# Expert products of U in three rounded products, with GpSimd making the low parts

## The reference, cut to what matters

```python
def peer(x, w_query, sub_keys, expert_u, expert_v):
    ...
        best_s, best_j = lax.top_k(cand_s, PK_TOPK)
        experts = jnp.take_along_axis(cand_i, best_j, axis=-1)
        gates = jax.nn.softmax(best_s, axis=-1).astype(xb.dtype)
        act = jax.nn.gelu(jnp.einsum('thkd,td->thk', expert_u[experts], xb), approximate=False)
        return jnp.einsum('thk,thkd->td', gates * act, expert_v[experts])
```

## Time and profile before

| | us |
|---|---|
| median of 3 runs | 5192.61 |
| lowest and highest | 5158.98, 5197.61 |
| span of the profiled execution | 5087.9 |
| U part, first gather to last row (in the span) | 2826 to 4254 |
| V part, first product to last | 4266 to 5058 |

### The profile page before, as it was taken

The page is one execution under the profiler, slowest core; times in us unless marked ns, Lnnn a source line. Parts: engine busy times, 40 slices in busy tenths (PEclk is TensorE's granted clock), DMA queues, the critical chain, the costliest instruction groups (busy, mean ns, idle before and its releaser), DMA issues. The chain is left out here.

```text
span 5087.9 us, 68117 instructions
## 1 busy us (share of the span) xinstructions
PE 4732.6 (93%) x27237; PEld 3798.3 (75%) x27237; DVE 3153.2 (62%) x4952; ACT 1249.9 (25%) x1562; POOL 1567.5 (31%) x1385
## 2 busy tenths in 40 slices
PE   8999999999978888899999899999999938899997
PEld 7999999999976555898789555555555526677776
DVE  2323443333436666433457588889778876888987
ACT  2212323233322222322354000000000003334433
POOL 0110000000014444000000222256655564788850
PEclk9999999999988899999999999999999969999998
DMA  5533333233339998524556899999999999999995
GB/s 192 200 141 115 99 107 108 94 111 102 102 110 344 352 355 301 185 106 173 174 206 224 324 421 418 405 410 394 386 395 397 395 387 355 411 408 407 409 407 199
DMA packets 346087, 1377.05 MB, mean 271 GB/s; under 512 B 85396, under 2 KB 128692, under 8 KB 220200
## 3 DMA queue, kind: packets, MB, share of 16 engines
q0 software_dynamic: 138464, 727.19, 35.7%
q1 hardware_dynamic: 176536, 613.34, 32.8%
q10 hardware_dynamic: 30768, 32.11, 1.9%
HBM read 1277.05 MB, written 111.66 MB: 273 GB/s over the span
## 5 line engine op out<-in xcount | busy, mean ns | idle before, releaser
L2262 PE MATMUL i_ps<-f_xT,i_ut 128*128 128x384 f32 x4096 | 1326.6, 487 | 83.6 <-DMA i_ut<-in_u_tiles 83.6
L2262 PEld LDWEIGHTS i_ps<-f_xT,i_ut 128*128 128x128 f32 x4096 | 779.9, 191 | 628.4 <-issue 89.1
L300 PE MATMUL a_acc<-a_xh,a_wh 128*128 128x288 f32 x3104 | 673.2, 299 | 19.1 <-DVE a_xl L526 13.7
L300 PE MATMUL a_acc<-a_xh,a_wl 128*128 128x288 f32 x3104 | 666.4, 296 | 0.0
L300 PE MATMUL a_acc<-a_xl,a_wh 128*128 128x288 f32 x3104 | 665.6, 296 | 0.0
L2674 POOL DMA_INDIRECT i_row<-in_expert_v,f_ei x320 | 481.6, 1505 | 245.2 <-DVE i_sum L2511 97.2
L2511 DVE SCALAR_TENSOR_TENSOR i_ps<-i_row,i_cf,i_ps 128x2048 f32<-128x2048 f32 x190 | 447.5, 2355 | 136.1 <-DMA i_row<-in_expert_v,f_ei 127.0
L300 PEld LDWEIGHTS a_acc<-a_xh,a_wh 128*128 128x128 f32 x3104 | 500.4, 189 | 30.6 <-issue 28.4
L300 PEld LDWEIGHTS a_acc<-a_xl,a_wh 128*128 128x128 f32 x3104 | 501.6, 189 | 0.0
L300 PEld LDWEIGHTS a_acc<-a_xh,a_wl 128*128 128x128 f32 x3104 | 501.4, 189 | 0.0
L2502 DVE CUSTOM_DVE_ANT_0 i_row<-i_row,i_ps 128x2048 f32<-128x2048 f32 x192 | 430.4, 2284 | 98.2 <-DMA i_row<-in_expert_u,f_ei 95.8
(11 more groups left out here) (372 smaller groups left out, 7342.7 us busy)
## 6 DMA issues: line engine op xcount, KB each, us to landing
i_ut<-in_u_tiles SPq DMA_DIRECT2D x128, 1024.0 KB, 9.6
i_ut<-in_expert_v SPq DMA_DIRECT2D x128, 1024.0 KB, 13.1
a_w<-in_w_in SPq DMA_DIRECT2D x97, 1024.0 KB, 5.0
f_w<-in_w_out SPq DMA_DIRECT2D x32, 1024.0 KB, 4.9
f_w<-in_w_query SPq DMA_DIRECT2D x32, 1024.0 KB, 5.2
tmp_Ha<-i_ho ACTq DMA_DIRECT2D x128, 192.0 KB, 9.1
tmp_uT<-a_out POOLq DMA_DIRECT2D x65, 288.0 KB, 2.3
tmp_Wd<-in_zeros SPq DMA_DIRECT2D x16, 1024.0 KB, 7.3
```

The source lines that it names most:

```text
L300: last = nc.tensor.matmul(acc[:, 2 * slot + h, 0:HALF], weights[:, wslot, k * P:(k + 1) * P], x[:, k, h * HALF:(h + 1) * HALF], start=(k = ...
L2262: last = nc.tensor.matmul(p_h[:, e % 2, 0:ND], ut[:, e % RU, k * P:(k + 1) * P], xT[:, k, :], start=(k == 0), stop=(k == KT - 1))
```

## The change

U's dense product is made like V's, as three rounded products. x is split once into `i_xh` (ACT) and `i_xl` (DVE). Of each U tile ACT makes the high part `i_uh` in two halves of 1024 columns (`split_u`, two buffers), and POOL subtracts it from the tile, in place: `i_ul` is the same memory as `i_ut` (`split_low`). PE waits for POOL's halves. POOL's subtractions for tile e stand in its queue behind gather 3(e - 1) + 1. To make room, row buffers go from eight to five and U slots from six to four, and the V part's buffers lie over those of the U part.

```diff
-    R = 8
+    R = 5
-    RU = 6
+    RU = 4
...
+        uh = sb("i_uh", [P, 2, KT * P], F32R)
+        ut, = over(("i_ut", [P, RU, KT * P], F32))
+        ul = sb("i_ul", [P, RU, KT * P], F32R)
...
                     if e < RV:
-                        sp.wait_ge(e_done, NE + (-6, -5, -2, -1)[e] + 1 + 4)
+                        sp.wait_ge(e_done, NE - RU + e + 1 + 4)
...
-                        if e == NE - 6:
+                        if e == NE - RU:
                             sp.wait_ge(routed, 4)
                             sp.wait_ge(placed, 16 * 2 * PICKS)
...
-                        pe.wait_ge(ut_in[e % RU], 16 * (e // RU + 1))
                         for k in range(KT):
-                            last = nc.tensor.matmul(p_h[:, e % 2, 0:ND], ut[:, e % RU, k * P:(k + 1) * P], xT[:, k, :],
-                                                    start=(k == 0), stop=(k == KT - 1))
+                            if k % 8 == 0:
+                                pe.wait_ge(ul_out, 2 * e + k // 8 + 1)
+                            if e == 0 and k % 4 == 0:
+                                pe.wait_ge(xl_out, k // 4 + 1)
+                            hi, lo = uh[:, e % 2, k * P:(k + 1) * P], ul[:, e % RU, k * P:(k + 1) * P]
+                            for t, (u, x) in enumerate(((hi, xh), (hi, xl), (lo, xh))):
+                                last = nc.tensor.matmul(p_h[:, e % 2, 0:ND], u, x[:, k, :], start=(k == 0 and t == 0),
+                                                        stop=(k == KT - 1 and t == 2))
...
                     nc.scalar.copy(ho[:, m, :], p_h[:, e % 2, 0:ND]).then_inc(h_out, 1)
+                    if e + 2 < NE:
+                        split_u(e + 2)
...
+                def split_u(e):
+                    act.wait_ge(ut_in[e % RU], 16 * (e // RU + 1))
+                    if e >= 2:
+                        act.wait_ge(e_done, e - 1 + 4)
+                    for h in range(2):
+                        part = slice(h * D // 2, (h + 1) * D // 2)
+                        nc.scalar.copy(uh[:, e % 2, part], ut[:, e % RU, part]).then_inc(uh_out, 1)
...
+                def split_low(e):
+                    for h in range(2):
+                        part = slice(h * D // 2, (h + 1) * D // 2)
+                        pool.wait_ge(uh_out, 2 * e + h + 1)
+                        nc.gpsimd.tensor_tensor(ul[:, e % RU, part], ut[:, e % RU, part], uh[:, e % 2, part], ALU.subtract
+                                                ).then_inc(ul_out, 1)
...
+                def splits(m):
+                    if m % 3 == 1:
+                        split_low(m // 3 + 1)
...
                 for k in range(PICKS):
                     gather(k, io["expert_u"], ei[:, 0, k:k + 1])
+                    if k == 0:
+                        split_low(0)
+                    splits(k)
...
                 for k in range(PICKS):
                     gather(first_v[0] + k, io["expert_v"], ei[:, 0, k:k + 1])
+                    splits(first_v[0] + k)
                     scatters(first_v[0] + k)
```

More of the change, by code:

```diff
@@ L2091, in peer @@
         tcol = sb("i_tcol", [P, 3])
[L2092 to L2096, removed]
+        vh, vl, gb = over(("i_vh", [P, 2, D], F32R), ("i_vl", [P, 2, D], F32R), ("i_gb", [P, 2, D], F32))
+        xl = sb("i_xl", [P, KT, ND], F32R)
+        ho = sb("i_ho", [P, 4, ND])
+        xh = sb("i_xh", [P, KT, ND], F32R)
+        uh = sb("i_uh", [P, 2, KT * P], F32R)
+        ut, = over(("i_ut", [P, RU, KT * P], F32))
+        ul = sb("i_ul", [P, RU, KT * P], F32R)
         row = sb("i_row", [P, R, D])
+        sb("i_x1_gap", [P, 512])
         sb("i_x1_room", [P, 2, D])
@@ L2115, in peer @@
         ut_in = [tl.sem(f"i_ut_in{k}") for k in range(RU)]
+        xh_out = tl.sem("i_xh_out")
+        xl_out = tl.sem("i_xl_out")
+        uh_out = tl.sem("i_uh_out")
+        ul_out = tl.sem("i_ul_out")
         e_done = tl.sem("i_e_done")
@@ L2178, in load_v @@
                     if e < RV:
-                        sp.wait_ge(e_done, NE + (-6, -5, -2, -1)[e] + 1 + 4)
+                        sp.wait_ge(e_done, NE - RU + e + 1 + 4)
                     else:
                         sp.wait_ge(vl_out, e - RV + 1)
-                    sp.dma_start(ut[:, (e + 2) % RV, :], v_rows[e // 2, e % 2]).then_inc(v_in[e % RV], 16)
+                    sp.dma_start(ut[:, e % RV, :], v_rows[e // 2, e % 2]).then_inc(v_in[e % RV], 16)
                 def store_y(j):
@@ L2208, in _ @@
                 tiles(SCORES_AT[3] + 1, 16)
-                load_v(0)
-                load_v(1)
-                sp.wait_ge(e_done, NE - 2 + 4)
+                for e in range(RV):
+                    load_v(e)
                 for i, name in enumerate(("ln2_g", "ln2_b")):
                     sp.dma_start(gb[:, i, :], io[name].to_broadcast([P, D])).then_inc(gb_in, 16)
-                load_v(2)
-                load_v(3)
                 sp.wait_ge(hi_out, 1)
@@ L2318, in evict, with split_x @@
                     nc.scalar.copy(ho[:, m, :], p_h[:, e % 2, 0:ND]).then_inc(h_out, 1)
+                    if e + 2 < NE:
+                        split_u(e + 2)
                     act.wait_ge(h_out, e + 1 + 2)
                     act.dma_start(dr["Ha"][e // 2, :, e % 2, :], ho[:, m, :]).then_inc(h_stored[m], 16)
+                def split_x(q):
+                    nc.scalar.copy(xh[:, 4 * q:4 * q + 4, :], xT[:, 4 * q:4 * q + 4, :]).then_inc(xh_out, 1)
+                def split_u(e):
[5 more added lines that the diff above has]
+                        nc.scalar.copy(uh[:, e % 2, part], ut[:, e % RU, part]).then_inc(uh_out, 1)
                 def gelus(u):
@@ L2340, in v_hi @@
                         act.wait_ge(v_done, e - 1)
-                    nc.scalar.copy(vh[:, e % 2, :], ut[:, (e + 2) % RV, :]).then_inc(vh_out, 1)
+                    nc.scalar.copy(vh[:, e % 2, :], ut[:, e % RV, :]).then_inc(vh_out, 1)
                 def square(j):
@@ L2355, in root @@
                     nc.scalar.activation(st[0:n, j, 8:9], st[0:n, j, 7:8], ACT.Sqrt).then_inc(root_out, 1)
+                for q in range(4):
+                    split_x(q)
+                split_u(0)
+                split_u(1)
                 for r in range(16):
@@ L2528, in v_lo @@
                     dve.wait_ge(vh_out, e + 1)
-                    v.tensor_tensor(vl[:, e % 2, :], ut[:, (e + 2) % RV, :], vh[:, e % 2, :], ALU.subtract).then_inc(vl_out, 1)
+                    v.tensor_tensor(vl[:, e % 2, :], ut[:, e % RV, :], vh[:, e % 2, :], ALU.subtract).then_inc(vl_out, 1)
                 def mean(j):
@@ L2603, in hooks @@
                         route(GATES_AT[c], 6)
+                for q in range(4):
+                    dve.wait_ge(xh_out, q + 1)
+                    v.tensor_tensor(xl[:, 4 * q:4 * q + 4, :], xT[:, 4 * q:4 * q + 4, :], xh[:, 4 * q:4 * q + 4, :], ALU.subtract
+                                    ).then_inc(xl_out, 1)
                 residual(0, 0)
@@ L2705, in _ @@
                     gather(P + k, io["expert_u"], ei[:, 4, k:k + 1])
+                    splits(P + k)
                     scatters(P + k)
@@ L2711, in _ @@
                     gather(first_v[4] + k, io["expert_v"], ei[:, 4, k:k + 1])
+                    if first_v[4] + k < 3 * P - 2:
+                        splits(first_v[4] + k)
                     scatters(first_v[4] + k)
```

## The result

| | us |
|---|---|
| before, median of 4 runs | 5185.73 (5158.98 to 5197.61) |
| after, median of 4 runs | 5350.63 (5342.26 to 5355.90) |
| ratio after/before, 95% interval | 1.0312 (1.0285 to 1.0339) |
| forecast | 5445 (5230 to 5610) |

What follows compares the result with a forecast made beforehand. The prediction took POOL's queue as pace maker between gathers 144 and 359, where it also scatters. Its terms, 25 + 106 + 121 - 20 + 15 + 5 = +252 us, added to the median 5192.6, gave 5445 us, range 5230 to 5610.

Steps and rivals of the forecast that it cites:

- m = 0 to 144: Gathers before any scatters: POOL's subtractions covered by waits for DVE; later third gather and less routing cover cost +25 us.
- 144 to 232: Gathers with 16 scatters to every 11: each of 8 groups grows 13.3 us to 57.2, +106 us.
- 232 to 359: Gathers with one scatter each: each of 8 groups of 16 grows 15.1 us to 71.7, +121 us.
- to V's first product: End of the U stage: four slots' tiles left instead of six, about 80 us for 102, -20 us.
- contention: POOL and DVE holding each other up in routing and gate sums: 32 times half a microsecond, +15 us.
- I take 5 us: POOL's wait for scatters to land, per group between gathers 144 and 359, assumed 5 us in both stretches.
- the rest, 104.7 us: Difference between the profiled span, 5087.9 us, and the runs' median, 5192.6, to which the change was added.
- Its own speed did not set the end: U stage before: PE ran ahead and waited 78.07 us for a U tile; the rows, through POOL, set the end.
- The cost of nothing that I gave PE's gain: U products: tiles 1.8 us shorter, 230 us over 128 tiles, counted as no gain since rows and DMA set the pace.
- the +40 of the bounds: V part with five row buffers: forecast +5 us, upper bound +40 if a third of the rows come 1 us late.
- Rival (a): POOL's waits swallow the cost: subtraction 1.1 to 1.2 us, scatter waits 2.5, about 5240 us; chance 0.14.
- (d): The forecast's chain with POOL subtractions of 3.1 us, 6.8 per tile: +144 us over the sum, 5600; chance 0.14.

Runs made afterwards that it cites:

- second profile: The kernel before, unchanged, profiled once more: span 5171.5 us, V's first product 1474 us after the first gather.
- the run with the low part in name only: The changed kernel with POOL subtracting 32 columns for 1024 and PE's third product taking the high part: 5187.18 us, ratio to before 1.0041.
- the run with two products: The changed kernel with PE leaving out low part of U times high part of x, every wait kept: 5327.03 us, ratio to before 1.0311.

## Why the prediction was right, and what was mis-sized

The mechanism held: POOL's queue sets the pace while it scatters, and most of the loss, 58 + 96 us by the second profile, lies between m = 144 and 359. The size was half too high, 252 for 165, and the range from +37 to +417 was wide enough to hold it. Of the signs named ahead, the subtraction of 2.4 us, PE's many waits (4.0 us on the mean) and V's length came out. Scatter waits of 5 us did not, and the DMA share was under 0.9 in the first of the two stretches only. The terms, against both profiles of before:

| term | forecast | by the first | by the second |
|---|---|---|---|
| m = 0 to 144 | +25 | +28 | +27 |
| 144 to 232 | +106 | +80 | +58 |
| 232 to 359 | +121 | +88 | +96 |
| to V's first product | -20 | -1 | -20 |
| V | +5 | -5 | -3 |
| contention | +15 | in the above | in the above |

The gather at 4151.57 in the earlier trace rows, taken for m = 359, is m = 358; 359 stands at 4154.14. The table's first profile is cut there, and the forecast's group of 56.6 us should have been 56.9.

**The groups.** 430/8 = 53.8 us for the forecast 57.2, and 544/8 = 68.0 for 71.7: together 57 us less. The pair costs 4.64 us for the forecast 4.8: each subtraction is longer (2.40 us for 2.1), but the second follows without the gap of 0.30 and the DMA issue after it comes 0.17 later. This term was right by two errors that cancel. The mis-sized term is the scatter wait: "I take 5 us" per group, and it was 23.7/16 = 1.5. 3.5 us times 16 groups is 56 of the 87 us by which the forecast was too high; the pairs' 12 too many are cancelled by 12 us of waits for DVE that it left out. The likely reason was in the same sentence: the longer a group, the more of its transfers have landed by its end. At DMA shares of 0.83 and 0.92 there is less of a queue to wait behind. Working from the pace instead gives the stage: 471 gathers and scatters (216 + 255) at 1.28 us and 71.7 pairs at 4.64 are 936 us; with 36 us of waits 972, for 974.

**The rest of the surplus** is 16 us from the state of before from which it was counted, 15 of contention counted beside groups that hold it already, and 8 in V (+5 for -3). Two terms point the other way: 2 us in m = 0 to 144, and 7 between the profiles' 158 and the runs' 165. The forecast took group lengths from one execution (351 and 453 us) that was fast in the first scatter part; the second profile has 372 and 448. One profile gave the terms and another population, the runs, gave the base.

**The step "the rest, 104.7 us, is what the median of the runs (5192.6) has beyond the span"** was wrong, and so was its reading as what the metric counts beyond the first and last instruction. The changed kernel's profiled execution took 5349.98 us with a span of 5348.3: 1.7 us lie around the span. By that the profiled execution of before took about 5090 us, 69 less than the fastest run. The 104.7 was mostly the luck of that execution. The forecast added its change to the median, so the sum was not hurt.

**"Its own speed did not set the end"** was only half true: in the second profile PE carries the chain. The cost of nothing that I gave PE's gain is right all the same, which the run with the low part in name only shows: with PE faster and POOL's queue almost as free as before, the rows end no sooner. Tiles took 8.4 us (48 products at 173 ns between starts) for the forecast 8.5.

**The start of the stage**: the third gather went out 15.4 us after the first for 2.6, so 13 later for the forecast 12. **The end of the stage** came out as worked by the second profile, 130 to 110 us, with fewer tiles behind the wait, and hardly moved by the first, 112 to 111. **V** lost nothing by its five buffers; the +40 of the bounds was far too much.

**Contention** I had priced as half a microsecond 32 times on POOL. On POOL it is 2.8 us over all subtractions, and the lengthened DMA issues of the U part come to about 18 us for 14 in the first profile of before. On DVE it is 69 us, in few and large pieces: 41 in 12 gate sums, 28 in nine small operations of the routing and the gates, the longest 4.98 us for 0.21. The gate sums, by line, in before and in the changed kernel (duration in ns min/median/max, first and last start, forms):

```profile
L2589 DVE SCALAR_TENSOR_TENSOR i_junk<-i_ed,f_gt x256: 340/347/404, 3340.5 to 3834.4; 128x128 f32<-128x128 f32 x128
```

```profile
L2615 DVE SCALAR_TENSOR_TENSOR i_junk<-i_ed,f_gt x256: 340/348/5598, 3428.2 to 4028.6; 128x128 f32<-128x128 f32 x128
```

The median stayed and the longest went from 0.40 to 5.60 us. It seems to have cost little, as DVE was busy only 0.78 and 0.75 of the two stretches; no run isolates it. Rival (a) had the short scatter wait but a subtraction of half the length, (d) the reverse; the truth took (a)'s wait with a subtraction near mine.

## What to carry over

Idle time on a queue's engine is worth something only up to the point where its own waits are used up: count the queue's fixed pace (instructions times spacing, plus what is added), compare it with the stretch, and let the waits shrink towards nothing before the stretch grows. Take the terms and the base from more than one execution of before, where stretches differ by 20 us and the end of the chain changes engine between them. Speeding up one of two engines that end together gives nothing by itself, and paying for it on a third makes that one the bound.

## What the runs showed of the hardware

A POOL subtraction takes 295 ns for 32 columns, 1304 for 512 and 2396 for 1024, so by an estimate from these 2.12 ns per column over some 0.23 us. The forecast's reading of two streams in turn (2 x 0.98 ns) was near.

POOL and DVE exclude each other in whole pieces. Around 4019 us DVE's second gate sum of a batch and POOL's pair above meet:

```profile
4019.01 5.47 DVE L2615 SCALAR_TENSOR_TENSOR i_junk<-i_ed,f_gt 128x128 f32<-128x128 f32 x1
```

An operation of 0.35 us ends at 4024.48, just behind the pair (4024.32): DVE got no turn between the two subtractions. Its record begins 0.57 us before the pair, while POOL issues a gather (4018.57 to 4019.55), as do the three others of over 5 us. 12 of the 16 batches met one so, for 0.9 to 5.6 us. DVE's dot products, with one operand in PSUM, were never touched: all 192 took 2273 to 2290 ns. The Trainium skill ("SBUF — State Buffer", Who interferes with whom) names just this pair, a DVE instruction with two SBUF inputs and a GpSimd one that reads SBUF; the trace agrees, and adds that the loser waits for the whole pair. The reverse happens too: a subtraction that began at 3619.28, while a routing operation of DVE ran (3618.48 to 3620.77), took 3.70 us for 2.38. Nor is it two inputs alone: of the nine small operations held, five were casts or operations with a scalar that read one tile, for 0.8 to 5.0 us. And POOL's DMA issue is held, as in the earlier trace rows: in the V part 119 gathers whose issue met a row sum or a split of DVE (two inputs in SBUF) took 2.29 us on the mean, the 7 others 0.94.

The granted clock fell with PE's pauses, from 0.95 to 0.85 in the first scatter part: 269 of its 1417 products follow the one before after 0.32 us, most others after 0.17, that is 1.2 GHz for 2.4. With PE off the bound it cost nothing, as the run with two products shows.
